# Moving long-convolution products and the mean step later, and reordering the last branch, in a two-layer trunk on one core

## The reference

```python
h = rmsnorm(x, norm_mix)
q, k, v, cglu, sc_b, sc_c, sc_h, gates = split(h @ w_in)
y_a = window_attention(q, k, v, sinks, bias) @ w_attn_out
ca, cb = split(cglu)
c = causal_dwconv(ca * sigmoid(cb), conv_dw) + conv_dw_bias      # 31 taps, 1024 channels
c = silu(layernorm(c))                                           # mean and variance over channels
y_b = c @ w_conv_out
y_c = (sc_b * causal_dwconv(sc_c * sc_h, sc_conv)) @ w_sc_out    # 3 taps
g = sigmoid(gates)                                               # three gates of width 1024
x = x + (g[0]*y_a + g[1]*y_b + g[2]*y_c) @ w_mix_out
```

## Time and profile before

| what | value |
|---|---|
| median of 3 runs (range) | 1150.75 us (1149.22 to 1153.69) |
| profiled execution, its own time | 1149.08 us |
| its span in the profile | 1147.3 us |
| busy PE / DVE / ACT / POOL | 1112.1 / 811.9 / 697.5 / 414.4 us |
| granted TensorE clock, mean | 0.996 |
| layer 0: attn_out, sc_out, conv_out | from 196.3, 239.8, 283.8 us |

### The profile page before, as it was taken

One profiled execution on the slowest core, in us unless ns is written; L12 is line 12 of the kernel. 1 busy time (PEld: TensorE's weight loads), 2 busy tenths in 40 slices (PEclk: granted clock), 3 DMA queues, 4 the chain that ended last, 5 costly groups with the idle time before them and its releaser, 6 DMA issues.

```text
span 1147.3 us, 19188 instructions
## 1 busy us (share of the span) xinstructions
PE 1112.1 (97%) x7190; PEld 1003.0 (87%) x7190; DVE 811.9 (71%) x1143; ACT 697.5 (61%) x1073; POOL 414.4 (36%) x405
## 2 busy tenths in 40 slices
PE   6999999999999999999999999999999999999997
PEld 5999889888798889889989988988887978998997
DVE  6887997977756554554898899888785655545555
ACT  5768987766645443444666788877574444334445
POOL 0587658783002000002228876778520200000012
PEclk9999999999999999999999999999999999999999
DMA  8565334555544554555335543345556455455441
GB/s 301 191 229 201 125 113 147 183 214 199 197 169 175 192 187 179 189 186 178 111 138 198 209 155 123 136 148 201 203 193 219 148 187 187 178 191 184 177 147 37
DMA packets 29350, 201.44 MB, mean 176 GB/s; under 512 B 3520, under 2 KB 3712, under 8 KB 5840
## 3 DMA queue, kind: packets, MB, share of 16 engines
q1 hardware_dynamic: 27648, 195.38, 47.7%
q0 software_dynamic: 1088, 4.74, 1.2%
q10 hardware_dynamic: 528, 0.15, 0.1%
HBM read 199.19 MB, written 3.69 MB: 177 GB/s over the span
## 4 chain that ended last, share of the span: by engine, by line
PE 49%; DVE 16%; ACT 12%; POOL 10%; DMA 7%; issue 5%; DVEq 0%; POOLq 0%; SPq 0%; ACTq 0%
POOL pacc L1476 10%; PE bank L406 8%; PE bank L408 8%; PE bank L407 8%; PE bank L345 7%; PE bank L346 7%; PE bank L347 7%; DMA w_raw<-in_wstream 6%; ACT w_hi L660 6%; DVE w_lo L1021 6%; ACT cprod L660 2%; DVE probs L1198 1%; DVE act_lo L1025 1%; PE bank L582 1%; PE bank L382 1%
## 5 line engine op out<-in xcount | busy, mean ns | idle before, releaser
L1021 DVE TENSOR_TENSOR w_lo<-w_raw,w_hi 128x2048 fp32r<-128x2048 f32 x183 | 432.2, 2365 | 228.0 <-ACT w_hi L660 215.2
L660 ACT ACTIVATE w_hi<-w_raw 128x2048 fp32r<-128x2048 f32 (+1 forms) x185 | 351.1, 1901 | 200.8 <-DMA w_raw<-in_wstream 79.7
L1476 POOL TENSOR_TENSOR pacc<-pacc,cprod 128x256 f32<-128x256 f32 x280 | 299.0, 1068 | 80.8 <-ACT cprod L660 43.5
L345 PE MATMUL bank<-h_hi,w_hi 128*128 128x256 f32 x832 | 241.8, 291 | 1.7 <-DVE w_lo L1021 0.5
L346 PE MATMUL bank<-h_lo,w_hi 128*128 128x256 f32 x832 | 236.7, 285 | 0.0
L347 PE MATMUL bank<-h_hi,w_lo 128*128 128x256 f32 x832 | 236.5, 284 | 0.0
L406 PE MATMUL bank<-w_hi,h_hi 128*128 128x512 f32 x544 | 214.6, 395 | 0.0
L408 PE MATMUL bank<-w_hi,h_lo 128*128 128x512 f32 x544 | 212.3, 390 | 0.0
L407 PE MATMUL bank<-w_lo,h_hi 128*128 128x512 f32 x544 | 212.1, 390 | 0.0
L1436 POOL TENSOR_TENSOR sqsum<-xs 128x256 f32<-128x256 f32 x6 | 3.9, 650 | 508.7 <-DVE xs L1323 458.5
L660 ACT ACTIVATE cprod<-cv,prms 128x256 f32<-128x256 f32 x310 | 141.0, 504 | 65.5 <-POOL pacc L1476 64.5
(11 more groups left out here) (174 smaller groups left out, 1442.2 us busy)
## 6 DMA issues: line engine op xcount, KB each, us to landing
w_raw<-in_wstream SPq DMA_DIRECT2D x183, 1024.0 KB, 4.9
rel_bias_rows<-rel_bias_by_distance POOLq DMA_DIRECT2D x1, 2560.0 KB, 19.4
bias<-rel_bias_rows POOLq DMA_DIRECT2D x1, 1536.0 KB, 11.3
xs<-in_x SPq DMA_DIRECT2D x2, 512.0 KB, 4.4
w_raw<-in_wstream SPq DMA_DIRECT2D x2, 512.0 KB, 7.7
out_y<-xs SPq DMA_DIRECT2D x4, 256.0 KB, 2.4
zacc<-in_p POOLq DMA_DIRECT2D x2, 256.0 KB, 3.5
prms<-in_prm SPq DMA_DIRECT2D x1, 328.0 KB, 10.3
```

The lines of the kernel that those rows point to most:

```text
L345: nc.tensor.matmul(o, wh, hi, start=first, stop=False, skip_group_check=True)
L660: return nc.scalar.activation(o, i, ACT.Identity, **kw)
L1021: nc.vector.tensor_tensor(w_lo[:, n % RING, :], w_raw[:, n % RAW_RING, :], f32(w_hi[:, n % RING, :]), ALU.subtract).then_inc(lo_ready, 1)
L1476: nc.gpsimd.tensor_tensor(o, a, cprod[:, n % PROD_RING, :], ALU.add).then_inc(pool_step, 1)
```

## The change

- Of the 155 products, the attention stage gets 4 a chunk instead of 6 (48 instead of 72, so 100 are made before attn_out). The remaining 55 are spread over twelve chunks, the eight of attn_out and the first four of sc_out, instead of 31 over eight.
- The mean matmul comes after the sixth chunk of sc_out, before its fourth group. ACT copies the mean in its step 6 (and squares four tiles there, four in step 7), DVE subtracts in its step 5. The variance matmul moves to between the two chunks of the first group of conv_out; root, reciprocal, silu, rounding and low parts move into conv_out steps 0, 1 and 2.
- conv_out has both gate groups first, then both weight groups (the weight stream is reordered to match), so that the convolution is read from the fifth chunk on. The second gate's sigmoids go to buffers of their own (`v_tok`, `kk`). The first half of the mix is transposed between the two chunks of the fourth group instead of within the third.

```diff
-CGLU_PRODUCTS, QKV_PRODUCTS, SC_PRODUCTS = 4, 4, 6
+CGLU_PRODUCTS, QKV_PRODUCTS, SC_PRODUCTS = 4, 4, 4
+LATE_CHUNKS = 12
-MEAN_AT, VAR_AT = 3, 6
+MEAN_AT = 5
...
+        late_gate_tok = lambda b: (v_tok, kk)[b][:, :, :].rearrange("p a b -> p (a b)")
...
-                branch("sc_out", sc_src, tiles_ready(sc_lo, L * DT), js=range(2))
+                branch("sc_out", sc_src, tiles_ready(sc_lo, L * DT), js=range(3))
                 pe.wait_ge(csum_step, L * 2 * (DT - 1) + DT - 1)
                 nc.tensor.matmul(psum[4][:, 0:SEQ], ones[:, :], sqsum[:, :], start=True, stop=True).then_inc(cmean_done, 1)
+                branch("sc_out", sc_src, js=range(3, 4))
...
-                branch("sc_out", sc_src, js=range(2, 4), mid=variance)
-                branch("conv_out", (act_hi, act_lo, 0), tiles_ready(conv_lo, L * DT), amid=lambda: turn_mix(0))
+                branch("conv_out", (act_hi, act_lo, 0), tiles_ready(conv_lo, L * DT), order=(0, 2, 1, 3),
+                       mid={0: variance, 3: lambda: turn_mix(0)})
...
+                def late_gates():
+                    for b in range(TB):
+                        wait_strip(act, L, S0["conv_out"] + 6 + b)
+                        nc.scalar.activation(late_gate_tok(b), psum[2 + b][:, :], ACT.Sigmoid).then_inc(bank_read[2 + b], 2)
...
+                def late_products(n):
+                    conv_products(before_attn + -(-(PRODUCTS - before_attn) * min(n, LATE_CHUNKS) // LATE_CHUNKS))
                 for j in range(DT):
                     after_chunk(C0["attn_out"] + j - 1)
                     branch_gates("attn_out", j)
-                    conv_products(before_attn + -(-(PRODUCTS - before_attn) * (j + 1) // DT))
+                    late_products(j + 1)
                 for j in range(DT):
                     after_chunk(C0["sc_out"] + j - 1)
-                    if j == MEAN_AT:
+                    if j == MEAN_AT + 1:
                         act.wait_ge(cmean_done, L + 1)
                         copy(mu[:, :], psum[4][:, 0:SEQ]).then_inc(mu_ready, 1)
...
                     branch_gates("sc_out", j)
+                    late_products(DT + j + 1)
...
-                    if j == 4:
+                    if j == 7:
                         round_mix(0)
...
+                    if j == 5:
+                        branch_product(S0["conv_out"] + 8, S0["conv_out"] // BANKS + 1, 0, gate_tok, 0, mix_ready)
+                    if j == 7:
                         low_mix(0)
+                        branch_product(S0["conv_out"] + 12, S0["conv_out"] // BANKS + 1, 1, late_gates, 2, mix_ready)
```

More of the change, by code:

```diff
@@ L528, in _, with branch @@
                           amid=(lambda: probs_transpose(j - 1)) if 0 <= j - 1 < QT else None)
-                def branch(name, src, ready=None, js=range(4), amid=None, mid=None):
+                def branch(name, src, ready=None, js=range(4), amid=None, mid=None, order=(0, 1, 2, 3)):
                     for i in js:
[L533 to L536, removed]
+                        s, n = S0[name] + 4 * i, order[i]
+                        tok_group(L, s, C0[name] + 2 * i, src if n % 2 else h_src, 2 * (i % 2),
+                                  L * USES + (S0[name] + 8 * (i // 2)) // BANKS + 1, ready=ready if n == 1 else None,
+                                  amid=amid if i == 3 else None, mid=mid.get(i) if mid else None)
                 def turn_mix(f):
@@ L891, in _ @@
                         nc.scalar.activation(rstd[:, :], psum[4][:, 0:SEQ], ACT.Sqrt, bias=eps[:, :]).then_inc(cstd_ready, 1)
-                    if j == VAR_AT + 1:
+                    if j == 1:
                         for t in range(DT):
                             conv_silu(t)
-                for j in range(DT):
-                    after_chunk(C0["conv_out"] + j - 1)
-                    if j == 0:
+                    branch_gates("conv_out", j if j < 5 else 0)
+                    if j == 2:
                         for t in range(DT):
                             round_conv(t)
-                    branch_gates("conv_out", j)
-                    if j == 4:
+                    if j == 3:
+                        late_gates()
+                    if j == 7:
                         round_mix(0)
@@ L1262, in _, with branch_product @@
                 low_sc(DT - 1)
[L1265 to L1269, removed]
+                def branch_product(s, use, f, gates, banks, final=None):
                     for b in range(TB):
[L1271 to L1275, removed]
+                        wait_strip(dve, L, s + 2 + b)
+                        if gates is gate_tok:
+                            dve.wait_ge(bank_read[b], L * USES + use + 2)
+                        else:
+                            dve.wait_ge(bank_read[2 + b], L * USES + use + 2)
+                        o, bank = mix_tok[:, b, f * 512:(f + 1) * 512], banks + b
+                        done = L * USES + use + 2 + (2 if final is mix_ready else 0)
+                        nc.vector.tensor_tensor(o if final is None else part_tok[b], psum[bank][:, :], gates[b],
+                                                ALU.mult).then_inc(bank_read[bank], 2)
                         if final is not None:
-                            dve.wait_ge(bank_read[2 + b], L * USES + s // BANKS + 3)
+                            dve.wait_ge(bank_read[bank], done)
                             nc.vector.tensor_tensor(o, o, part_tok[b], ALU.add).then_inc(final, 1)
@@ L1286, in low_mix, with late_taps @@
                             act_hi[:, t:t + 2, :].rearrange("p a b -> p (a b)"), mix_lo)
+                def late_taps(n):
+                    taps(min(EARLY_TAPS + ATTN_TAPS * n, len(DVE_TAPS)))
+                late_gates = [late_gate_tok(0), late_gate_tok(1)]
                 for j in range(DT):
                     after_chunk(C0["attn_out"] + j - 1)
[L1290 to L1291 removed]
+                    if j % 4 == 3:
+                        branch_product(S0["attn_out"] + 2 * (j - 1), (S0["attn_out"] + 2 * (j - 3)) // BANKS + 1, j // 4, gate_tok, 2)
+                    late_taps(j + 1)
                 for j in range(DT):
@@ L1296, in _ @@
                             dve.wait_ge(bank_read[2 + b], L * USES + S0["sc_out"] // BANKS + 1)
-                    branch_product("sc_out", j, mix_added)
+                    if j % 4 == 3:
+                        branch_product(S0["sc_out"] + 2 * (j - 1), (S0["sc_out"] + 2 * (j - 3)) // BANKS + 1, j // 4, gate_tok, 2,
+                                       mix_added)
+                    late_taps(DT + j + 1)
                     if j == MEAN_AT:
@@ L1301, in _ @@
                             nc.vector.tensor_tensor(cv[:, t, CPAD:], cv[:, t, CPAD:], mu[:, :], ALU.subtract).then_inc(dev_ready, 1)
-                    if j == VAR_AT:
+                for j in range(DT):
+                    after_chunk(C0["conv_out"] + j - 1)
+                    if j == 0:
+                        dve.wait_ge(mix_added, L * 4 + 4)
                         dve.wait_ge(cstd_ready, L + 1)
@@ L1561, in _weight_stream @@
         for g, w in ((g0, w_attn), (g2, rows("w_sc_out")), (g1, rows("w_conv_out"))):
-            for f in range(TB):
-                strips += [side(g, 4 * f), side(w, 4 * f)]
+            strips += [side(g, 0), side(w, 0), side(g, 4), side(w, 4)] if g is not g1 else [side(g, 0), side(g, 4), side(w, 0), side(w, 4)]
         strips += [cols(rows("w_mix_out"), t) for t in range(DT)]
```

15 lines of the change are left out of this document (8 added, 7 removed).

## The result

The changed kernel takes 1166.92 us (median of 4 runs, 1164.63 to 1168.88) against 1150.38 us of the kernel before in the same sessions: a ratio of 1.0136, 95% interval 1.0114 to 1.0158. Its profiled execution has a span of 1164.7 us, 17.4 us more than before.

A forecast was written before the change was run, and what follows sets the result against it. PE's own work and waits were taken as the bound (busy 1112.1 of 1147.3 us). Attention -1.8, mix -2.4, mean wait +20 and clock +3 gave +18.8 on 1149.1, 1167.9; with 1.7 for the median 1169.6 us, range 1154 to 1181.

The forecast's parts named there:

- POOL's capacity of four adds a chunk: In attn_out while PE runs: four adds take POOL 5.39 us against a chunk of 5.44, so it can do no more.
- The pattern of one long and three short adds: POOL's late adds at L1476: one of 2.61 us, held up by DVE's weight subtraction, then three of 0.74 or 0.75.
- The earlier start: POOL's late adds, from attn_out on, begin 5 us earlier (bounds 0 and 8.3), the last ending at 275.5 us.
- The wait at the mean: PE at the mean matmul in sc_out waits for POOL's sums, 10 us a layer, 20 us in all.
- Weights under the lag: ACT's weight preparation in sc_out runs 7 us late, with 12 us of lag covered; nothing counted.
- the rival, a wait before L406: PE waits for weights ahead of the mean if ACT's lag passes 12 us: 6 us a layer more, about 1182; chance 0.09.
- The clock: PE behind each wait at the mean runs at half clock: 1.5 us a wait (1.0 to 3.4), 3 us in all.
- The attention stage: Products moved out of it cut PE's waits before the probabilities' transposes: 1.8 us gained for both layers, at most 3.5.
- The order of the last branch: In conv_out, waits before the mix's transposes (L546) go: -2.4 us; the second half is covered by under 1 us.
- From the mean to the convolution's group: Six chunks from the mean matmul to the group reading it, as before: no wait, bounds 0 and 2 us a layer.
- The sum: Whole kernel: -1.8 - 2.4 + 20 + 3 = +18.8 us against the profiled execution of 1149.1 us.
- no wait at the mean: POOL's adds in attn_out and sc_out at 1.13 us or less, so only the gains remain: 1146.6 us; chance 0.09.

The follow-up runs named there:

- x4: Changed kernel with DVE writing the low weights by a one-source operation (raw weights times a constant), leaving their low part out: 1130.59 us, ratio 0.9827.
- x1: Changed kernel with the products where they were before (6 per attention chunk, the last 31 over eight chunks): 1149.29 us, ratio 0.9998.
- x2: Changed kernel with 5 products per attention chunk instead of 4, so 43 late products over twelve chunks: 1152.59 us, ratio 1.0017.
- x9: Changed kernel with the mean matmul after sc_out's fourth group instead of before it, two chunks later again: 1162.13 us, ratio 1.0092.
- x3: Kernel before with 4 products per attention chunk and nothing else, so 55 late products over eight chunks: 1178.44 us, ratio 1.0240.
- x7: Changed kernel with 5 products per attention chunk and the 43 late ones over eight chunks: 1160.88 us, ratio 1.0089.
- x6: Changed kernel with 5 products per attention chunk and the 43 late ones over ten chunks: 1149.43 us, ratio 0.9981.
- x13: Changed kernel with products as before (6 per attention chunk, the rest over eight), mean's copy and mix's first half ahead of weight work: 1146.32 us, ratio 0.9955.
- x11: x6 with the mean's copy ahead of the weight rounding and the mix's first half ahead of the weight operation: 1144.73 us, ratio 0.9942.
- x12: x7 with ACT's copy of the mean ahead of its weight rounding: 1157.53 us, ratio 1.0049.

## Why the prediction was right

- **POOL's capacity of four adds a chunk** held on the average: 1.34 us an add against 1.35 taken, in an unbroken row, 4.05 adds in a chunk; x4 shows that the stretch comes from DVE's operation. The pattern of one long and three short adds did not keep: there are fewer subtractions than chunks in this stretch, and some have four short adds between them.
- **The earlier start** of the late adds was taken as 5 us (202.5). Their unbroken run began at 200.65. PE was earlier by a like amount: it began attn_out at 194.1 instead of 196.3 us, having waited less in the attention stage, and wanted the mean at 270.5, not at 272.5. The last add ended at 273.2, not at 275.5. Both errors cancel in the wait, which is luck.
- **The wait at the mean**, 10 us a layer forecast, measured 10.1. Its two parts were off and cancel too: the adds left when PE came took 2.7 us and not 2.0, the seven sums 7.3 and not 8.0. x1 (products back, no wait) and x2 (fewer, 2.6 us a layer) show that the added adds make it, x9 that deferring the matmul moves three quarters of it to the next step.
- **Weights under the lag** cost nothing, as counted. But the price put on the rival, a wait before L406, is where the sum was blind: x3 shows that wait (15.3 us), x7 shows the same lag as a wait at the variance.
- **The clock** was undersized: 1.5 us a wait taken, 2.3 found, since it stayed at 0.50 for 4.9 us behind the wait instead of 3.4, and nearly half of the work was lost in them (11 of 23 matmuls) where the row had 9 of 30. It lies inside the bounds of 1.0 and 3.4 us a wait.
- **The attention stage** gained 3.0 us, of which I had taken 1.8.
- **The order of the last branch**: the 2.4 us at the mix's transposes went as forecast. That the following steps were covered was true in the changed kernel only; x1 and x6 had 1.9 us before mix_out, by a reader of the first half that the prediction did not list.
- **From the mean to the convolution's group** PE did not wait, as forecast. But the stall ahead of it made the room: without it x6 waits 2.0 us at the variance.
- The sum, +18.8 us, came out at +17.4 in the profiled executions and +16.5 in the medians.

The rival "no wait at the mean" failed on its own point: adds at 1.13 us were needed, 1.34 were found. Left open is what sets how long the clock stays low behind a wait (x13 has 6.6 us behind one of 2.2), and the 1.1 us not placed.

## What to carry to other kernels

An engine that looks 83% busy in a stage can be full: read the pattern of its single operations beside the partner engine's before moving work to it. When a late result is awaited by a deferred instruction, the deferral is worth only the reserve of the steps behind it; find the next one in the chain and what stands in front of it in its queue. Small copies that PE's statistics hang on belong ahead of bulk work that may wait for a DMA: two such swaps took 4 to 5 us off here (x6 to x11); with ACT further behind, one took off 3.4 us and left 9.3 us of waits (x12).

## What the runs showed of the hardware

An add of 128x256 on POOL took 0.74 us alone and 2.6 us when DVE's subtraction of two 128x2048 tiles in SBUF ran; with a one-source DVE operation of 1.23 us the longest was 1.76 us. DVE's taps, which read one operand from PSUM, left the adds at 0.74 us (taps from 231.20 to 233.25 us, adds at 232.01 and 232.90 in the changed kernel). The granted clock stayed at 0.50 for 4.9 us behind a wait of 10.1 us in which it had fallen already, for 3.4 us behind one of 2.2 us in the earlier trace rows, and for 6.6 us behind another of 2.2 us in x13, where PE did 33 matmuls against 60 in the next 6.8 us. So here the time at half clock did not grow with the wait alone. x2's waits of 2.6 us drew a stretch of 3.4 us in both layers. Removing 5.2 us of waits there (x6) was worth only about 3 us, since other waits had been hidden behind them and two stretches at half clock came in the attention stage instead.
